# Local attention's scores from stacked high and low query parts, transposed two tiles ahead, and a weight's split and the conv's parts placed otherwise

## The chip, the cores and the metric

One Trainium2 chip, one of its cores. The metric is the device time of one execution in microseconds (us), given as a median over runs. Five engines work side by side in the core: TensorE (PE: matmuls and transposes; PEld is its weight load), VectorE (DVE), ScalarE (ACT), GpSimd (POOL) and SyncE (SP, which issues most DMAs). They meet at semaphores only.

## What is computed

Two transformer blocks, one behind the other, in float32. The change sits in the second block, between its input product and its output product:

```python
h = modulate(rmsnorm_2(x, g_mix[l]), sh1, sc1)
q, k, v, bg, cg, hv = jnp.split(h @ w_in[l], SPLIT_POINTS, axis=-1)
q = apply_rope(q.reshape(bsz, seq, N_HEADS, HEAD_DIM), cos, sin)      # 8 heads of 64
k = apply_rope(k.reshape(bsz, seq, N_KV_HEADS, HEAD_DIM), cos, sin)   # 2 heads of 64
att = windowed_attention(q, k, v, k_c, v_c, sink[l])  # 256 context keys, latent keys with |i-j| <= 128
conv = short_conv_mixer(bg, cg, hv, conv_w[l])        # bg * conv3(cg * hv)
x = x + gt1 * (jnp.concatenate([att, conv], axis=-1) @ w_out[l])
```

The 1024 tokens are 8 tiles of 128. A query tile sees 256 context keys, its own tile and the tile on each side: 640 keys for tiles 1 to 6, 512 for tiles 0 and 7. Four query heads share one key head.

## The kernel before

Every engine has its own instruction stream, written out by hand, so the order on an engine is the order of the code; waits are semaphores.

**Products in parts.** A float32 product is made of three passes in the type fp32r: each operand is split into a high part (ACT copies it to fp32r) and a low part (DVE subtracts the high part from the original), and `mm3` (L425 to L429) adds high*high, high*low and low*high. Weights come as blocks of 1024x512 into `raw`; `split_hi` (L402) makes `WH` in four pieces on ACT, `split_lo` (L417) makes `WL` in four pieces on DVE. There is one `WH` and one `WL`, so a piece is overwritten only when the last tile of the product before has used it (`w_used`). Activations lie as `AH` and `AL`.

**The input product of block two** runs as `gemm_tokens(B_I2, T_Q2)` for the queries (8 tiles), `gemm_tokens(B_I2 + 1, T_KV)` for keys and values (10 tiles, two of them context) and `gemm_pair` for the parts of the short convolution (T_CG, T_HV, T_BG). On DVE `rotate_tile` (L1656) rotates 8 query tiles (r 0 to 7) and 10 key tiles (r 8 to 17) into a two-deep buffer `QR`; beside the products `rot_transpose` (L2208) transposes them on TensorE and `rot_copy` (L1170) stores them on ACT: queries as `QT2` (two heads stacked per column block), keys as `KZ4`, each key head twice with zeros in the other 64 rows, so that one product over 128 rows gives one head. A tile of `QR` is free again when its transposes are done, and in `rotate_tile` DVE waits for that.

**The attention** (PE L2266 to L2322, ACT L1210 to L1234, DVE L1736 to L1769) is one loop over v, one head of one tile per turn. On TensorE turn v holds: the transposes of head v-2's probabilities (L2278, 5 of them, 4 in tiles 0 and 7); the scores of head v (L2287 over the context keys, L2288 over the own tile, L2292 over a side tile with L2293 for its mask) in plain float32; for v = 2 mod 8 the transposes of a tile's inverse sums (L2301); and a quarter of the product of probabilities and values (L2317). DVE takes the maximum (L1743, L1745), ACT the exponential (L1220). The transposed probabilities go through one pair of PSUM banks and are copied out by ACT for even v and by DVE for odd v (`probs_copy`, L570). At v = 6 mod 8 (from 14) DVE scales a finished tile's output out of PSUM (L1764).

**Between the two**, on DVE: `split_lo(B_W2)` for the output weight (L1727), the last of the products with bg (L1731), and `AL` of the convolution (L1734); on ACT `split_hi(B_W2)` (L1204) and `AH` of it (L1207), and a wait until DVE's part is done (L1209) before the first head.

Of the kernel before, what the change touches and what calls it, by code (L numbers as in the profile page):

```python
# [102 lines left out]
def build(nc, x, mem, positions, norm_mix_w, w_in, conv_w, conv_b, conv_ln_w, conv_ln_b, ret_gn_w, w_out,  # L103
# [123 lines left out]
    QT2 = at("w_q_T", [P, 4, S], F32, O_R + 32 * K + 512)  # L227
    KZ4 = at("w_k_T", [P, 4, CTX + S], F32, O_R + 48 * K + 512)
# [65 lines left out]
    with ExitStack() as stack:  # L294
# [107 lines left out]
        def split_hi(b, off=0, width=512):  # L402


            for j in range(4):
# [11 lines left out]
        def split_lo(b, off=0, width=512):  # L417

            for j in range(4):
# [124 lines left out]

        def key_slot(j):
            return 2 + j if j < NT else j - NT
# [64 lines left out]
        def residual_pe(b, n0, ni):  # L611
# [28 lines left out]
            sem("xa_" + s) for s in ("scores", "max", "exp", "probs", "probs_T", "copied", "out", "hi", "lo"))  # L640
# [5 lines left out]
        rt_tp, rt_cp, kz_zero = sem("rot_transposed"), sem("rot_copied"), sem("k_zeroed_then_slots")  # L646
# [113 lines left out]
        def _(pool):  # L760
# [114 lines left out]
            pool.wait_ge(x_saved, 16 * NT)  # L875
            pool.wait_ge(nm_xn, N_CTX)
            pool.memset(KZ4[64:128, 0:4:2, :], 0.0).then_inc(kz_zero, 1)
            pool.memset(KZ4[0:64, 1:4:2, :], 0.0).then_inc(kz_zero, 1)
# [6 lines left out]
            pool.memset(AFFALL[:, :, :], -1.0).then_inc(u2_pad, 1)  # L885
# [63 lines left out]
        def _(act):  # L949
# [220 lines left out]
            def rot_copy(r):  # L1170

                act.wait_ge(rt_tp, r + 1)
                ps = BK[4 + r % 4]
                if r < 8:
                    act.activation(QT2[:, :, tok(r)], ps.rearrange("p (c n) -> p c n", c=4), ACT.Copy).then_inc(rt_cp, 1)
                    return
                act.wait_ge(kz_zero, 2)
                i_ = tok(key_slot(r - 8))
                act.activation(KZ4[0:64, 0, i_], ps[0:64, 0:P], ACT.Copy)
                act.activation(KZ4[0:64, 2, i_], ps[0:64, P:2 * P], ACT.Copy)  # L1180
                act.activation(KZ4[64:128, 3, i_], ps[64:128, 0:P], ACT.Copy)
                act.activation(KZ4[64:128, 1, i_], ps[64:128, P:2 * P], ACT.Copy).then_inc(rt_cp, 1)

            for r in range(15):
                if r == 2:
                    norm_hi(N_CTX, CTH[:, :, tok(0)])
                if r == 3:
                    split_hi(B_I2 + 1)
                if r == 4:
                    norm_hi(N_CTX + 1, CTH[:, :, tok(1)])  # L1190
                rot_copy(r)
            for m in range(8):
# [7 lines left out]
                if m < 3:  # L1200
                    rot_copy(15 + m)
            split_hi(B_I2 + 3)
            split_hi(B_I2 + 4)
# [107 lines left out]
        def _(dve):  # L1311
# [344 lines left out]
            def rotate_tile(r):  # L1656
                n = (T_Q2 if r < 8 else T_KV - 8) + r
                dve.wait_ge(acc_ready, n + 1)
                if r >= 2:
                    dve.wait_ge(rt_tp, r - 1)  # L1660
                if r >= 1:
                    dve.wait_ge(acc_dve, freed(n)[1] - 1)
                q = QR[:, r % 2, :]
                if r < 8:
# [3 lines left out]
                if r == 8:  # L1668
                    dve.wait_ge(kz_zero, 2)
# [815 lines left out]
```

## Time and profile before

| | us |
|---|---|
| median of 3 runs | 2669.22 (2668.21 to 2670.24) |
| the profiled execution | 2671.51 |
| its span in the profile | 2669.9 |
| input product of block two, attention, up to the output product | some 1490 to 1874 of the span |
| attention alone, first transposes to the output product | 1703.6 to 1874.2 |

The profiled execution's own time is 1.6 us over its span and 2.3 us over the median. The profile says, for one execution, when every instruction ran and what released it. A row of its timeline has the start, the duration, the engine, the line of the kernel and the operation with the names of its tiles; behind "x" stands how many instructions are merged, and in brackets how long the engine had been idle and what ended that. A float32 matmul shows as two MATMULs, an fp32r one and a transpose as one. Matmuls are pipelined, so the distance between two starts, and not the duration, is what one costs.

### The profile page before, as it was taken

The page shows a single profiled execution, that of the slowest core. Times are in us where ns is not written, and L with a number is a line of the kernel's source. Part 1 is how long each engine was busy: PE and PEld are TensorE (multiplying, and loading weights), DVE is VectorE, ACT ScalarE, POOL GpSimd, SP SyncE. Part 2 cuts the span into 40 slices and gives each one's busy share as a digit, 9 for nine tenths or more (in the row PEclk, how much of TensorE's full clock was granted, in tenths as well). Part 3 has the DMA queues.
Part 4 walks back from the last instruction along what each step waited for, and adds up shares of the span by engine and source line. Part 5 has one row for each costly group of instructions (what it writes and reads, how often), then busy time and mean ns, then how long its engine had stood idle before and what let it go on. Part 6 is the DMA issues. An engine that isn't in the chain of part 4 may idle for free. (4 is left out here: it accounts for less than half of the span.)

```text
span 2669.9 us, 30052 instructions
## 1 busy us (share of the span) xinstructions
PE 2528.8 (95%) x11886; PEld 1989.0 (74%) x11886; DVE 1460.4 (55%) x1924; ACT 925.3 (35%) x1480; POOL 203.2 (8%) x224
## 2 busy tenths in 40 slices
PE   6999899999999999999999999899985999999996
PEld 5787578878888787878878888777774766677663
DVE  5999745224344564445446733566357656655562
ACT  4233534334231212112214321444152545544452
POOL 1000320000000000000000100000112011010100
PEclk9999889999999999999999999899986999999998
DMA  4111022220011232323230410200255999999996
GB/s 144 58 45 44 32 87 72 95 95 9 32 66 61 80 110 83 101 85 110 79 110 32 166 32 16 79 1 1 99 211 209 340 359 366 370 374 359 359 360 220
DMA packets 116260, 370.53 MB, mean 139 GB/s; under 512 B 6293, under 2 KB 15557, under 8 KB 116160
## 3 DMA queue, kind: packets, MB, share of 16 engines
q1 hardware_dynamic: 94688, 293.63, 29.6%
q0 software_dynamic: 21472, 75.51, 9.0%
q8 instruction: 70, 1.15, 0.2%
q14 instruction: 30, 0.25, 0.0%
HBM read 343.89 MB, written 25.26 MB: 138 GB/s over the span
## 5 line engine op out<-in xcount | busy, mean ns | idle before, releaser
L427 PE MATMUL banks<-act_hi,w_hi 128*128 128x512 f32 x960 | 376.6, 392 | 12.1 <-DVE act_lo L541 5.6
L1900 DVE TENSOR_TENSOR expert_w_lo<-expert_w,expert_w_hi 128x2048 fp32r<-128x2048 f32 x120 | 269.3, 2287 | 210.7 <-ACT expert_w_hi L1268 210.5
L429 PE MATMUL banks<-act_hi,w_lo 128*128 128x512 f32 x960 | 374.4, 390 | 0.0
L428 PE MATMUL banks<-act_lo,w_hi 128*128 128x512 f32 x960 | 374.4, 390 | 0.0
L1268 ACT ACTIVATE expert_w_hi<-expert_w 128x2048 fp32r<-128x2048 f32 x128 | 237.6, 1904 | 125.4 <-DMA expert_w<-in_w_gate 76.3
L414 ACT ACTIVATE w_hi<-w_raw 128x1024 fp32r<-128x1024 f32 x152 | 156.8, 1060 | 345.2 <-PE banks L429 345.1
L427 PE MATMUL banks<-w_hi,act_hi 128*128 128x512 f32 (+1 forms) x640 | 247.4, 387 | 10.0 <-DVE w_lo L421 6.3
L421 DVE TENSOR_TENSOR w_lo<-w_raw,w_hi 128x1024 fp32r<-128x1024 f32 x152 | 181.3, 1223 | 136.3 <-ACT w_hi L414 132.0
L429 PE MATMUL banks<-w_hi,act_lo 128*128 128x512 f32 (+1 forms) x640 | 244.7, 382 | 0.0
L428 PE MATMUL banks<-w_lo,act_hi 128*128 128x512 f32 (+1 forms) x640 | 244.2, 382 | 0.0
L427 PEld LDWEIGHTS banks<-act_hi,w_hi 128*128 128x128 f32 x960 | 180.8, 188 | 52.7 <-DVE act_lo L541 5.7
L429 PEld LDWEIGHTS banks<-act_hi,w_lo 128*128 128x128 f32 x960 | 180.7, 188 | 37.9
L2393 PE MATMUL banks<-expert_w,expert_hidden_T 128*128 128x512 f32 x480 | 208.5, 592 | 0.0
L428 PEld LDWEIGHTS banks<-act_lo,w_hi 128*128 128x128 f32 x960 | 180.9, 188 | 36.9
L427 PE MATMUL banks<-expert_w_hi,expert_rows_T_hi 128*128 128x512 f32 x512 | 203.6, 398 | 4.2 <-DVE expert_rows_T_lo L1904 4.2
L427 PE MATMUL banks<-w_hi,hidden_hi 128*128 128x512 f32 x512 | 201.3, 393 | 2.8 <-DVE w_lo L421 2.8
L429 PE MATMUL banks<-expert_w_hi,expert_rows_T_lo 128*128 128x512 f32 x512 | 201.6, 394 | 0.0
L428 PE MATMUL banks<-expert_w_lo,expert_rows_T_hi 128*128 128x512 f32 x512 | 201.2, 393 | 0.0
L428 PE MATMUL banks<-w_lo,hidden_hi 128*128 128x512 f32 x512 | 199.4, 390 | 0.0
L429 PE MATMUL banks<-w_hi,hidden_lo 128*128 128x512 f32 x512 | 199.3, 389 | 0.0
L1612 DVE TENSOR_TENSOR x_tokens<-x_tokens,banks 128x512 f32<-128x512 f32 x128 | 87.6, 686 | 166.8 <-PE banks L429 165.5
L2393 PEld LDWEIGHTS banks<-expert_w,expert_hidden_T 128*128 128x128 f32 x480 | 90.1, 190 | 107.7 <-issue 107.6
(382 smaller groups left out, 3892.0 us busy)
## 6 DMA issues: line engine op xcount, KB each, us to landing
expert_w<-in_w_gate SPq DMA_DIRECT2D x32, 2048.0 KB, 9.8
expert_w<-in_w_up SPq DMA_DIRECT2D x32, 2048.0 KB, 9.9
expert_w<-in_w_down SPq DMA_DIRECT2D x32, 2048.0 KB, 7.9
ada_w<-in_w_ada POOLq DMA_DIRECT2D x48, 512.0 KB, 4.2
w_raw<-in_mlp_up_w SPq DMA_DIRECT2D x16, 1024.0 KB, 5.4
w_raw<-in_mlp_down_w SPq DMA_DIRECT2D x16, 1024.0 KB, 5.1
w_raw<-in_w_in SPq DMA_DIRECT2D x10, 1024.0 KB, 5.3
w_raw<-in_w_in SPq DMA_DIRECT2D x18, 512.0 KB, 6.2
```

What stands on the lines that cost most here:

```text
L414: nc.scalar.activation(WH[:, 2 * j:2 * j + 2, 0:width], raw[:, half, 2 * (j % 2):2 * (j % 2) + 2, 0:width], ACT.Copy).then_inc(w_hi, 1)
L421: nc.vector.tensor_tensor(WL[:, 2 * j:2 * j + 2, 0:width], raw[:, j // 2, 2 * (j % 2):2 * (j % 2) + 2, 0:width], WH[:, 2 * j:2 * j + 2, 0: ...
L427: nc.tensor.matmul(o_, lh, rh, start=start, stop=False)
L428: nc.tensor.matmul(o_, lh, rl, start=False, stop=False)
L429: return nc.tensor.matmul(o_, ll, rh, start=False, stop=stop)
L1268: act.activation(EWH[slot][:, 2 * j:2 * j + 2, :], EW[slot][:, 2 * j:2 * j + 2, :], ACT.Copy).then_inc(w_hi, 1)
L1612: dve.tensor_tensor(xs, xs, acc(n), ALU.add).then_inc(acc_dve, 1)
L1900: dve.tensor_tensor(EWL[slot][:, c, :], EW[slot][:, c, :], EWH[slot][:, c, :], ALU.subtract).then_inc(w_ready, 1)
L2393: m = pe.matmul(PAIR[pair][:, 512 * half:512 * (half + 1)], lhs[:, k, :], EW[slot + k // 4][:, k % 4, 512 * half:512 * (half + 1)], start= ...
```

## The change

**Scores.** The rotated queries stay as rows (`QRT`). For each tile ACT copies them to fp32r (`query_hi`) and DVE subtracts (`query_lo`) into `QST`, in which each head's high and low parts stand side by side, 64 columns each. TensorE transposes that (`query_transpose`), so that a head's stationary operand has the high part in 64 rows and the low part in the other 64; ACT copies it into the free columns of `AH` and `AL` (`query_copy2`). Keys are split when they are rotated: `KHH` holds the high part twice, stacked, `KLO` the low part once. The scores are then two fp32r passes per stretch of keys: the stacked query against `KHH` (128 rows) and the query's high part against `KLO` (64 rows). The stretches are the 256 context keys, two neighbouring tiles (256 keys), and for tiles 1 to 6 a third tile (128 keys).

**Order.** Tiles 0 and 1 of the queries are prepared beside the last conv product, tile t + 2 within the attention of tile t. The context's transposes move into the query product, keys are transposed one tile sooner, zeroing of `KZ4` on POOL goes. The output weight's split is made in pieces at v = 4 to 11, the conv's parts in two halves, one before the first head and one at v = 2.

```diff
+        def query_parts(t, kv):
+            hi, lo = (slice(0, AD), slice(AD, P)) if kv == 0 else (slice(AD, P), slice(0, AD))
+            return QST[:, t % 2, 4 * kv:4 * kv + 4, hi], QST[:, t % 2, 4 * kv:4 * kv + 4, lo]
...
-            pool.wait_ge(c2_lo, 4)
+            pool.wait_ge(c2_lo, 2)
+            pool.memset(AFFALL[:, :, :], -1.0).then_inc(u2_pad, 1)
+            pool.wait_ge(qs_tp, QS0 + 2 * NT)
             row(GT1[:, :], mod_d[0, 2 * D:3 * D], mod_in)
...
+            def query_hi(t):
+                act.wait_ge(acc_dve, freed(T_Q2 + t)[1])
+                if t >= 2:
+                    act.wait_ge(qs_tp, QS0 + 2 * (t - 1))
+                for kv in range(2):
+                    i_ = act.activation(query_parts(t, kv)[0], query_rows(t)[:, 4 * kv:4 * kv + 4, :], ACT.Copy)
+                i_.then_inc(qs_hi, 1)
+            def query_copy2(t, kv, bank):
+                act.wait_ge(qs_tp, QS0 + 2 * t + kv + 1)
+                act.activation((AL if kv else AH)[:, 0:4, tok(t)], BK[bank].rearrange("p (c n) -> p c n", c=4),
+                               ACT.Copy).then_inc(qs_cp, 1)
...
-            split_hi(B_W2)
-            act.wait_ge(acc_dve, freed(T_BG + 7)[1])
-            for c in range(4):
-                act.activation(AH[:, 4 + c, :], C2[:, c, :], ACT.Copy).then_inc(c2_hi, 1)
-            act.wait_ge(c2_lo, 4)
+            act.wait_ge(acc_ready, T_BG + 6)
+            for t in range(2):
+                for kv in range(2):
+                    query_copy2(t, kv, 4 + 2 * t + kv)
+            conv_hi(0)
+            act.wait_ge(acc_ready, T_BG + 8)
+            conv_hi(1)
             for v in range(64 + 15):
+                if v == 2:
+                    act.wait_ge(c2_lo, 2)
+                if v in (4, 6, 8, 10):
+                    split_hi(B_W2, js=((v - 4) // 2,))
+                if v % 8 == 5 and v < 48:
+                    query_hi(v // 8 + 2)
+                if v % 8 in (0, 2) and 8 <= v < 56:
+                    t = v // 8 - 1
+                    query_copy2(t + 2, v % 8 // 2, 6 + (t + 1) % 2)
...
+            def query_lo(t):
+                dve.wait_ge(qs_hi, QS0 + t + 1)
+                for kv in range(2):
+                    hi, lo = query_parts(t, kv)
+                    i_ = dve.tensor_tensor(lo, query_rows(t)[:, 4 * kv:4 * kv + 4, :], hi, ALU.subtract)
+                i_.then_inc(qs_lo, 1)
...
             for v in range(64 + 16):
+                if v == 2:
+                    conv_lo(1)
+                if v in (5, 7, 9, 11):
+                    split_lo(B_W2, js=((v - 5) // 2,))
+                if v % 8 == 6 and v < 48:
+                    query_lo(v // 8 + 2)
...
             for v in range(64 + 11):
+                if v % 8 in (7, 1) and 7 <= v < 50:
+                    t, kv = (v - 7) // 8, (v - 7) % 8 // 2
+                    if t >= 1:
+                        pe.wait_ge(at_on, t)
+                    if kv == 1:
+                        pe.wait_ge(qs_cp, QS0 + 2 * (t + 2) + 1)
+                    query_transpose(t + 2, kv, 6 + (t + 1) % 2)
...
-                    pe.matmul(ps[:, 0:CTX], q, kz[:, 0:CTX], start=True, stop=True)
-                    m = pe.matmul(ps[:, CTX:CTX + P], q, kz[:, CTX + t * P:CTX + (t + 1) * P], start=True, stop=True)
-                    sides = ([(t - 1, 0)] if t > 0 else []) + ([(t + 1, 1)] if t < NT - 1 else [])
-                    for n, (kt, side) in enumerate(sides):
-                        dst = ps[:, CTX + P * (n + 1):CTX + P * (n + 2)]
-                        pe.matmul(dst, q, kz[:, CTX + kt * P:CTX + (kt + 1) * P], start=True, stop=False)
-                        m = pe.matmul(dst, IDB[:, :], MKB[:, side, :], start=False, stop=True)
+                    for dst, key, n in spans:
+                        beside = [i for i, kt in enumerate(near) if kt != t and dst <= CTX + P * i < dst + n]
+                        pe.matmul(ps[:, dst:dst + n], q, KHH[:, kv, key:key + n], start=True, stop=False, skip_group_check=True)
+                        m = pe.matmul(ps[:, dst:dst + n], q[part, :], KLO[part, key:key + n], start=False, stop=not beside,
+                                      skip_group_check=True)
+                        for i in beside:
+                            m = pe.matmul(ps[:, CTX + P * i:CTX + P * (i + 1)], IDB[:, :], MKB[:, int(near[i] > t), :], start=False,
+                                          stop=True, skip_group_check=True)
```

**How it moves instructions.** The lines of the changed kernel have their own numbers. First DVE, at the end of the query product, where it stands before the split of the key weight. Before:

```order
L1652 TENSOR_TENSOR rotated<-rotary_tmp 128x8x32 [waits dve_link]
L1653 TENSOR_TENSOR rotated<-rotary_tmp 128x8x32
L421 TENSOR_TENSOR w_lo<-w_raw,w_hi 128x1024 [waits w_hi_made] x4
L1648 TENSOR_TENSOR rotary_tmp<-banks,consts_sb 128x256 [waits acc_free_dve,rot_transposed,acc_ready]
L1649 TENSOR_TENSOR rotary_tmp<-banks,consts_sb 128x256
L1650 TENSOR_TENSOR rotary_tmp<-banks,consts_sb 128x256
L1651 TENSOR_TENSOR rotary_tmp<-banks,consts_sb 128x256
L1652 TENSOR_TENSOR rotated<-rotary_tmp 128x8x32 [waits dve_link]
L1653 TENSOR_TENSOR rotated<-rotary_tmp 128x8x32
L541 TENSOR_TENSOR ctx_lo<-banks,ctx_hi 128x4x128 [waits nm_hi] x2
```

and changed:

```order
L1693 TENSOR_TENSOR w_q_rows<-rotary_tmp 128x8x32 [waits dve_link]
L1694 TENSOR_TENSOR w_q_rows<-rotary_tmp 128x8x32
L545 TENSOR_TENSOR ctx_lo<-banks,ctx_hi 128x4x128 [waits nm_hi] x2
L425 TENSOR_TENSOR w_lo<-w_raw,w_hi 128x1024 [waits w_hi_made] x4
L1689 TENSOR_TENSOR rotary_tmp<-banks,consts_sb 128x256 [waits acc_free_dve,acc_ready]
L1690 TENSOR_TENSOR rotary_tmp<-banks,consts_sb 128x256
L1691 TENSOR_TENSOR rotary_tmp<-banks,consts_sb 128x256
L1692 TENSOR_TENSOR rotary_tmp<-banks,consts_sb 128x256
L1693 TENSOR_TENSOR w_q_rows<-rotary_tmp 128x8x32 [waits dve_link]
L1694 TENSOR_TENSOR w_q_rows<-rotary_tmp 128x8x32
```

The second context tile's low part has moved ahead of the split, and a query's rotation waits for no transposes any more.

Next DVE at the entry of the attention. Before:

```order
L1731 TENSOR_TENSOR short_conv_out<-short_conv_out,banks 128x512 [waits acc_ready] x4
L421 TENSOR_TENSOR w_lo<-w_raw,w_hi 128x1024 [waits w_hi_made] x4
L1731 TENSOR_TENSOR short_conv_out<-short_conv_out,banks 128x512 [waits acc_ready]
L1734 TENSOR_TENSOR act_lo<-short_conv_out,act_hi 128x1024 [waits short_conv_hi] x4
L1743 TENSOR_REDUCE w_max<-banks 128x1 [waits wa_scores]
L1745 TENSOR_SCALAR w_minus_max<-w_max,minus_sink 128x1 [waits dve_link]
```

and changed:

```order
L1791 TENSOR_TENSOR short_conv_out<-short_conv_out,banks 128x512 [waits acc_ready] x4
L1782 TENSOR_TENSOR act_lo<-short_conv_out,act_hi 128x4x512 [waits short_conv_hi]
L1791 TENSOR_TENSOR short_conv_out<-short_conv_out,banks 128x512 [waits acc_ready]
L1810 TENSOR_REDUCE w_max<-banks 128x1 [waits wa_scores]
L1812 TENSOR_SCALAR w_minus_max<-w_max,minus_sink 128x1 [waits dve_link]
L1810 TENSOR_REDUCE w_max<-banks 128x1 [waits wa_scores]
L1812 TENSOR_SCALAR w_minus_max<-w_max,minus_sink 128x1 [waits dve_link]
L1782 TENSOR_TENSOR act_lo<-short_conv_out,act_hi 128x4x512 [waits short_conv_hi]
```

The split of the output weight no longer stands ahead of the last product with bg, and of the conv's low part only half stands ahead of the first maximum.

Last TensorE in the loop, at a turn v = 7 mod 8. Before:

```order
L2278 MATMUL banks<-consts_sb,w_probs 128x128 [waits wa_copied_act,wa_exp]
L2278 MATMUL banks<-consts_sb,w_probs 128x128 x4
L2287 MATMUL banks<-w_k_T,w_q_T 128x256 [waits wa_exp]
L2288 MATMUL banks<-w_k_T,w_q_T 128x128
L2292 MATMUL banks<-w_k_T,w_q_T 128x128
L2293 MATMUL banks<-masks_bf_65,identity_bf_64 128x128
L2292 MATMUL banks<-w_k_T,w_q_T 128x128
L2293 MATMUL banks<-masks_bf_65,identity_bf_64 128x128
L2317 MATMUL banks<-w_probs_T,w_v 64x256 x2
```

and changed:

```order
L2315 MATMUL banks<-consts_sb,w_q_parts_f_135 128x128 [waits xa_max_then_query_lo,wa_normed]
L2315 MATMUL banks<-consts_sb,w_q_parts_f_135 128x128 x3
L2345 MATMUL banks<-consts_sb,w_probs 128x128 [waits wa_copied_act,wa_exp]
L2345 MATMUL banks<-consts_sb,w_probs 128x128 x4
L2363 MATMUL banks<-w_k_hi_T,act_lo 128x256 [waits wa_exp]
L2364 MATMUL banks<-w_k_lo_T,act_lo 128x256
L2363 MATMUL banks<-w_k_hi_T,act_lo 128x256
L2364 MATMUL banks<-w_k_lo_T,act_lo 128x256
L2367 MATMUL banks<-masks_bf_65,identity_bf_64 128x128
L2363 MATMUL banks<-w_k_hi_T,act_lo 128x128
L2364 MATMUL banks<-w_k_lo_T,act_lo 128x128
L2367 MATMUL banks<-masks_bf_65,identity_bf_64 128x128
```

Four float32 products became six fp32r passes, and ahead of them stand four transposes that wait for DVE's scaling of the finished tile (`wa_normed`).

## Rows read from the trace of the kernel before

**Rows 1.** The profile page's first line on engines: busy time, share, instructions.

```profile
PE 2528.8 (95%) x11886; PEld 1989.0 (74%) x11886; DVE 1460.4 (55%) x1924; ACT 925.3 (35%) x1480; POOL 203.2 (8%) x224
```

**Rows 2.** TensorE's waits from 1490 to 1930 us: total, times, longest.

```profile
PE banks L2278 <- ACT w_probs L1220: 5.8, 3, 4.6
PE banks L427 <- DVE w_lo L421: 3.6, 1, 3.6
```

**Rows 3.** Timeline at the start of the key product (start, us, engine, line).

```profile
1521.58 1.06 ACT L414 ACTIVATE w_hi<-w_raw 128x1024 fp32r<-128x1024 f32 x1 [0.24 <-PE banks L429]
...
1522.07 0.42 DVE L1648 TENSOR_TENSOR rotary_tmp<-banks,consts_sb 128x256 f32<-128x256 f32 x1 [2.82 <-PE banks L2218]
...
1524.20 4.62 DVE L421 TENSOR_TENSOR w_lo<-w_raw,w_hi 128x1024 fp32r<-128x1024 f32 x4
...
1526.61 0.57 PE L427 MATMUL banks<-w_hi,act_hi 128*128 128x256 f32 x1
...
1530.13 0.28 PE L428 MATMUL banks<-w_lo,act_hi 128*128 128x256 f32 x1
...
1530.25 0.28 PE L429 MATMUL banks<-w_hi,act_lo 128*128 128x256 f32 x1
```

**Rows 4.** Timeline at the entry of the attention, all engines.

```profile
1694.14 0.68 DVE L1731 TENSOR_TENSOR short_conv_out<-short_conv_out,banks 128x512 f32<-128x512 f32 x1
...
1694.97 1.19 PE L2287 MATMUL banks<-w_k_T,w_q_T 128*128 128x256 f32 x2 [3.10 <-DVE short_conv_out L1731]
...
1695.94 4.63 DVE L1734 TENSOR_TENSOR act_lo<-short_conv_out,act_hi 128x1024 fp32r<-128x1024 f32 x4 [1.12 <-ACT act_hi L1207]
...
1701.50 1.28 ACT L1220 ACT_TABLE_LOAD   x1 [2.75 <-DVE w_minus_max L1745]
...
1703.62 1.11 PE L2278 MATMUL banks<-consts_sb,w_probs 128*128 128x128 f32 x4 [4.59 <-ACT w_probs L1220]
```

**Rows 5.** Timeline of TensorE over one head in tile 2.

```profile
1750.00 0.22 PE L2293 MATMUL banks<-masks_bf,identity_bf 128*128 128x128 bf16 x1
...
1750.73 0.76 PE L2278 MATMUL banks<-consts_sb,w_probs 128*128 128x128 f32 x5
...
1751.34 0.60 PE L2287 MATMUL banks<-w_k_T,w_q_T 128*128 128x256 f32 x2
...
1752.69 0.65 PE L2317 MATMUL banks<-w_probs_T,w_v 128*64 128x256 f32 x4
...
1753.28 0.76 PE L2278 MATMUL banks<-consts_sb,w_probs 128*128 128x128 f32 x5
```

**Rows 6.** Timeline of DVE and ACT over the heads beside it.

```profile
1750.26 0.82 DVE L1743 TENSOR_REDUCE w_max<-banks 128x1 f32<-128x640 f32 x1 [1.47 <-PE banks L2293]
...
1751.12 0.21 DVE L1745 TENSOR_SCALAR w_minus_max<-w_max,minus_sink 128x1 f32<-128x1 f32 x1
...
1751.37 0.79 ACT L1220 ACTIVATE w_probs<-banks,w_minus_max 128x640 f32<-128x640 f32 x1 [0.90 <-DVE w_minus_max L1745]
...
1754.08 0.70 ACT L1212 ACTIVATE w_probs_T<-banks 128x640 f32<-128x640 f32 x1 [1.83 <-PE banks L2278]
...
1754.68 0.79 ACT L1220 ACTIVATE w_probs<-banks,w_minus_max 128x640 f32<-128x640 f32 x1
...
1756.34 0.68 DVE L1764 TENSOR_TENSOR w_out_T<-banks,w_inverse_sums_T 128x512 f32<-128x512 f32 x1
```

**Rows 7.** Timeline in tile 0, where TensorE waited for an exponential.

```profile
1709.58 0.68 ACT L1220 ACTIVATE w_probs<-banks,w_minus_max 128x512 f32<-128x512 f32 x1
...
1710.41 0.66 PE L2278 MATMUL banks<-consts_sb,w_probs 128*128 128x128 f32 x4 [0.42 <-ACT w_probs L1220]
```

**Rows 8.** Busy time by stretch there: PE, PEld, DVE, ACT, POOL, then granted clock.

```profile
1708.00:1710.00 2.00, 1.99 (x16) 1.56 (x15) 1.04 (x3) 1.25 (x4) 0.00 (x0) 1.00 0.00 0
```

**Rows 9.** Timeline of TensorE: the transposes of heads 8 and 56.

```profile
1720.99 0.77 PE L2278 MATMUL banks<-consts_sb,w_probs 128*128 128x128 f32 x5
...
1850.01 0.66 PE L2278 MATMUL banks<-consts_sb,w_probs 128*128 128x128 f32 x4
```

More of the change, by code:

```diff
@@ L400, in sp_load, with split_hi @@
             nc.sync.dma_start(raw[:, half, :, 0:width], src).then_inc(w_raw[half], 16)
-        def split_hi(b, off=0, width=512):
-            for j in range(4):
+        def split_hi(b, off=0, width=512, js=range(4)):
+            for j in js:
                 half = j // 2
@@ L415, in split_hi, with split_lo @@
                                      ACT.Copy).then_inc(w_hi, 1)
-        def split_lo(b, off=0, width=512):
-            for j in range(4):
+        def split_lo(b, off=0, width=512, js=range(4)):
+            for j in js:
                 nc.vector.wait_ge(w_hi, off * 4 + 4 * b + j + 1)
@@ L639, in build @@
         xa_s, xa_m, xa_e, xa_p, xa_t, xa_pt, xa_o, xa_hi, xa_lo = (
-            sem("xa_" + s) for s in ("scores", "max", "exp", "probs", "probs_T", "copied", "out", "hi", "lo"))
+            sem("xa_" + s) for s in ("scores", "max_then_query_lo", "exp_then_query_hi", "probs", "probs_T_then_query_T",
+                                     "copied_then_query_copied", "out", "hi", "lo"))
+        qs_lo, qs_hi, qs_tp, qs_cp, QS0 = xa_m, xa_e, xa_t, xa_pt, 16
         u_sq, u_hi, u_lo = sem("hidden_squared"), sem("hidden_hi_made"), sem("hidden_lo_made")
@@ L1168, in _, with key_copy @@
                     norm_hi(N_B2 + t - 2, a_hi(t - 2))
[L1170 to L1191, printed above, removed]
+            def key_copy(j):
+                act.wait_ge(rt_tp, j + 1)
+                if j == 0:
+                    act.wait_ge(x_saved, 16 * NT)
+                    act.wait_ge(nm_xn, N_CTX)
+                ps = BK[4 + j % 4]
+                i_ = tok(key_slot(j))
+                act.activation(KHH[:, :, i_], ps[:, 0:2 * P].rearrange("p (v n) -> p v n", v=2), ACT.Copy)
+                act.activation(KLO[:, i_], ps[:, 2 * P:3 * P], ACT.Copy).then_inc(rt_cp, 1)
+            norm_hi(N_CTX, CTH[:, :, tok(0)])
+            norm_hi(N_CTX + 1, CTH[:, :, tok(1)])
+            split_hi(B_I2 + 1)
+            for j in range(8):
+                key_copy(j)
             for m in range(8):
@@ L2264, in _, with query_transpose, first_queries2 @@
             gemm_pair(B_I2 + 3, T_BG, 256, False, True)
-            gemm_pair(B_I2 + 4, T_BG + 4, 0, True, True)
-            pe.wait_ge(rt_cp, 18)
+            def query_transpose(t, kv, bank):
+                pe.wait_ge(qs_lo, QS0 + t + 1)
+                for n in range(4):
+                    m = pe.transpose(BK[bank][:, n * P:(n + 1) * P], QSF[:, t % 2, 4 * kv + n, :], IDN)
+                m.then_inc(qs_tp, 1)
+            def first_queries2(m):
+                if m == 1:
+                    pe.wait_ge(rt_cp, 10)
+                    for t in range(2):
+                        for kv in range(2):
+                            query_transpose(t, kv, 4 + 2 * t + kv)
+            gemm_pair(B_I2 + 4, T_BG + 4, 0, True, True, after=first_queries2)
             pe.wait_ge(acc_dve, freed(T_BG + 7)[1])
+            pe.wait_ge(qs_cp, QS0 + 4)
             for v in range(64 + 11):
+                if v % 8 in (7, 1) and 7 <= v < 50:
+                    t, kv = (v - 7) // 8, (v - 7) % 8 // 2
+                    if t >= 1:
+                        pe.wait_ge(at_on, t)
+                    if kv == 1:
+                        pe.wait_ge(qs_cp, QS0 + 2 * (t + 2) + 1)
+                    query_transpose(t + 2, kv, 6 + (t + 1) % 2)
                 if 2 <= v <= 65:
@@ L2299, in _ @@
                         pe.wait_ge(at_on, t)
+                    if t + 2 < NT:
+                        pe.wait_ge(qs_cp, QS0 + 2 * t + 6)
                     for n in range(4):
@@ L2312, in _ @@
                             pe.wait_ge(at_on, t - 1)
-                    keys = [0, 1, 2 + t] + ([1 + t] if t > 0 else []) + ([3 + t] if t < NT - 1 else [])
+                    keys = [0, 1] + [2 + kt for kt in local_tiles(t)]
                     more = len(keys) - 4
```

164 lines of the change are left out of this document (85 added, 79 removed).

## The prediction

> **What bounds the kernel now.** The page's engine line [rows 1] has TensorE busy for 95% of the span, so time can come from its work or from its few stops. The table of waits for the part that the change touches [rows 2] shows the stops: 5.8 us for exponentials, nearly all of it once, at the entry of the attention, and 3.6 us for the low part of a weight. The timelines give the rest. At the key product [rows 3] ACT had the last high part done at 1522.64, but DVE began the low parts only at 1524.20: it had stood idle for 2.82 us until a transpose on TensorE freed the rotated buffer, and then rotated first. After the stop TensorE ran at half its clock: from 1526.61 to 1530.13 are 17 passes, 0.21 us each, where the next one costs 0.12. At the entry [rows 4] the last product with bg stood behind a weight's split, then the conv's low parts (4.63 us) stood ahead of the first maximum, and the first transposes came at 1703.62, though the product had ended at 1691.87.
>
> Within the attention one turn takes 2.55 us of TensorE's stream [rows 5]: transposes 0.61, scores 1.35 (with masks and the switch to the next line), values 0.59. It is unbroken there. The loop behind it [rows 6] has mask to maximum 0.26, maximum to the next step 0.86, that 0.21, and an ACT copy that starts 0.80 behind the transposes, with the next exponential 0.60 behind the copy. From an exponential's start to the transposes it releases [rows 7] are 0.83 for 512 keys, so 0.94 for 640 (the exponential takes 0.79 instead of 0.68) [rows 6, 7]. From head 8 to head 56 pass 129.0 us [rows 9], 21.5 for each of six full tiles.
>
> All sums are against the profiled execution, 2671.5; the median is 2.3 lower, and that I take off at the end.
>
> **1. Start of the key product: -4.1.** The rotation of a query no longer waits for transposes, and both context tiles' low parts stand ahead of the split. DVE then follows ACT piece by piece and is done one piece (4.62/4 = 1.2) after 1522.64, at 1523.9. TensorE finds the first piece ready: the 3.6 goes [rows 2], and with it the half clock, 17 x 0.21 - 17 x 0.12 = 1.5. New: 0.4 until the fourth piece, and 0.6 because keys are transposed one tile sooner, with two rotations (2.2 each, six steps of some 0.4 [rows 3]) and the key's own still queued on DVE.
>
> **2. Transposes beside the products: -0.7.** 32 of queries and 20 of keys go, 30 of keys and 16 of queries come, six fewer at 0.12 (0.61 for five) [rows 5]. Splitting keys on DVE replaces two small copies by two operations of similar size; each key tile has some 3 us of TensorE over it and DVE needs about 2.2, so this costs nothing; were that cover gone, 10 x 0.3. POOL's zeroing had ended long before; its two row loads now wait for the last query transposes, still 50 us ahead of their use. SP's load of the last weight half starts some 15 us later, 150 us ahead of its use: nothing.
>
> **3. Entry of the attention: -7.5.** The last product with bg starts when the matmul ends, 1691.9 instead of 1694.14, and TensorE 0.83 later [rows 4], 1692.7. The first maximum waits for no conv part: it and its successor are done at 1694.5. ACT does half of the conv's high part first (2048 elements, two of the 1.06 [rows 3], to 1694.6), then the 1.28 of table load and the 0.83 [rows 7]: transposes at 1696.7, 6.9 sooner. Behind it stand new pieces: 2.3 of conv on DVE before the third maximum (half of 4.63), and from v = 4 to 11 four splits of 1.06 on ACT and 1.2 on DVE, plus the first query tile's parts. Walked through turn by turn, they fill idle time of both engines for the most part and delay four turns by 0.3 to 0.7; shorter scores give back a little more. I take 7.5 at head 8; bounds 5.5 and 8.5.
>
> **4. Full tiles: -7.** A head's scores become four fp32r passes over 256 keys at 0.12 [rows 3], two over 128, one mask at some 0.06 and the last mask with the switch at 0.15 (1750.00 to 1750.15) [rows 5]. No row shows an fp32r pass over 128 columns. From below it is half of 0.12; from above it is the float32 rate, 1.35 - 0.21 over five blocks of 128 = 0.23. I take 0.11, the row it is nearest to: a transpose, also 128 columns behind a load of its own weights, at 0.12. Scores are then 0.48 + 0.22 + 0.06 + 0.15 = 0.91, and TensorE's turn 2.11 (bounds 2.01 and 2.35).
>
> TensorE does not get all of it. In even turns ACT copies, then takes the exponential that the next transposes need: 0.80 + 0.60 + 0.94 = 2.34. So four odd turns take 2.11, two even ones 2.34, and two are longer by a double share of values (some 0.42), one of them also by the transposes of the inverse sums (0.48) and a wait for them of 0.2: 8.44 + 4.68 + 2.53 + 3.21 = 18.9 a tile. To this come two groups of four query transposes, 0.48 each. That at v = 1 mod 8 lies partly in ACT's turn and costs 0.25. That at v = 7 mod 8 waits for DVE to scale the finished tile out of the same bank. From the start of the turn that is 0.61 + 0.76 + 0.26 + 0.86 + 0.21 + 0.04 + 0.68 = 3.42, with a hop 3.5, where TensorE arrives at 2.53: a new wait of 0.95, and 0.48 behind it. It falls in five tiles: 5 x (0.25 + 1.43) = 8.4. Six tiles: 113.4 + 8.4 = 121.8 against 129.0. The bounds of the 128-column pass make it 118 or 130.5. The parts of the queries on ACT and DVE (some 1.9 and 0.9 a tile) stand where either engine waits 0.7 and more for scores; uncovered they would cost 2.8 x 5 = 14.
>
> For the narrow pass there is also a rule in the Trainium skill, TensorE: Matmul & The Clock Gate, under Back-to-back issue gap: streams of load and matmul pairs sustain about 81 ns each at 128 columns. By it scores would be 0.06 shorter and the gain 2 us larger. The transposes here cost 120, so the sum stays with the row.
>
> **5. Last tile: -1.5.** Its heads have no third block; by the same rates scores shrink by some 0.37, and four of eight turns are TensorE's. The tail behind it is not touched.
>
> **Sum:** 4.1 + 0.7 + 7.5 + 7 + 1.5 = 20.8. 2671.5 - 20.8 = 2650.7, and 2.3 less on the median: **2648.5**.
>
> **Rivals.**
> *Narrow passes at the float32 rate* (0.23): the full tiles give nothing, rather -1.5 back. For it: no row at 128 columns. Against: the 256-column passes run at one column per cycle, and nothing [rows 3] hints at a change. Time 2648.5 + 8.5 = 2657.
>
> *ACT and DVE as the new bound.* Parts of queries, splits and the scaling meet in the same turns, transposes wait for both, and a full tile stays at about 21.5. For it: even turns are ACT's already in my sum. Against: DVE sits idle 1.47 and ACT 1.83 between operations [rows 6], more than is added to a turn. Time 2648.5 + 7 = 2655.5; if the entry's pieces don't hide either, 2659.
>
> *Waits overlap better:* the scaling is ready when TensorE arrives, narrow passes at 0.06: 4.8 + 3.6 more, 2640.
>
> *Slower: half clock in the attention.* TensorE's turn gets stops it does not have now, 0.23 in even turns and 0.95 once a tile. If the granted clock falls to 1.2 GHz there, a turn of 2.11 doubles to some 4, a full tile costs 34 instead of 20.3, and six of them 82 more: 2730. It decides from a quarter of the attention at half clock, since 20.8/82 is that. Against it: in tile 0, in the two microseconds before a stop of 0.42 [rows 7] and after others like it, the clock granted was 1.00 [rows 8]; for it: stops of 3.6 and 4.6 were followed by half clock [rows 3, 4]. The Trainium skill speaks against the change here: TensorE: Matmul & The Clock Gate, A second HAM failure mode, says that a TensorE which idles briefly between groups of matmuls, cycling through PSUM banks, swings between full and half clock. By that rule the time is this rival's; the trace of tile 0 does not agree with it.
>
> *The change does nothing:* what TensorE saves, another wait takes, 2669. It needs both the entry and the loop to fail, which share no cause.
>
> **How the numbers follow.** Chances: forecast 0.52, narrow passes 0.12, ACT and DVE 0.20, better overlap 0.08, half clock 0.04, nothing 0.04. The likeliest case's own range, from the entry's bounds and a 128-column pass of 0.06 to 0.13, is 2643 to 2654. The range for 8 in 10 takes in the two cases above it and most of the one below: 2640 to 2660. A measurement of this kernel tells about 0.2% (5.3 us) from no change. All cases but the last two lie below 2663.9: faster 0.92, same 0.04, slower 0.04.
>
> **What would show it.** Step 1: no wait for the low part at the key product, granted clock 1.00 through it, DVE's split ending some 1.3 behind ACT's. Step 3: the first transposes some 5 us behind the end of the last bg product, where it was 11.8. Step 4: narrow passes 0.11 apart, scores 0.91, odd turns near 2.1, even near 2.3, and once a tile TensorE idle some 0.95, released by the scaling on DVE. Wrong: scores over 1.1 (narrow passes), turns over 2.5 with TensorE waiting for exponentials or copies (ACT and DVE), a granted clock under 0.95 in full tiles (half clock), or a key product that still stops.

## The result and the profile after

The kernel became slower. Its median is 2715.07 us (2713.05 to 2717.88, 4 runs) against 2669.73 (2668.21 to 2671.43, 4 runs) of the kernel before on the same chip: ratio 1.0173, 95% interval 1.016 to 1.0186. Forecast were 2648.5 us, range 2640 to 2660, and 0.92 for faster. The profiled execution took 2717.88 us, its span is 2716.3, 46.4 more than the 2669.9 of before.

The page of the changed kernel, engine line and granted clock in 40 slices:

```profile
PE 2581.0 (95%) x11800; PEld 2002.4 (74%) x11800; DVE 1468.8 (54%) x1936; ACT 930.3 (34%) x1482; POOL 193.6 (7%) x222
...
PEclk9999889999999999999999999599996999999998
```

TensorE's share is still 95% [rows 1], with more busy time, and one slice of the clock stands at 5. The waits of TensorE for the same part as [rows 2]:

```profile
PE banks L2315 <- DVE w_out_T L1831: 3.0, 4, 0.8
PE banks L431 <- DVE act_lo L1835: 2.3, 1, 2.3
PE banks L2345 <- ACT w_probs L1261: 2.1, 2, 1.3
PE banks L2378 <- DVE w_inverse_sums L1825: 1.0, 1, 1.0
PE banks L2363 <- DVE short_conv_out L1791: 0.8, 1, 0.8
PE banks L431 <- DVE w_lo L425: 0.3, 1, 0.3
```

The two waits that the prediction wanted gone are gone: 3.6 for the low part became 0.3, 5.8 for exponentials became 2.1. TensorE waits less than before and yet needs longer, so the time is in what it executes. The timeline at the start of the key product, the place of [rows 3]:

```profile
1523.07 2.52 DVE L425 TENSOR_TENSOR w_lo<-w_raw,w_hi 128x1024 fp32r<-128x1024 f32 x2 [0.19 <-ACT w_hi L418]
1523.28 1.06 ACT L418 ACTIVATE w_hi<-w_raw 128x1024 fp32r<-128x1024 f32 x1 [0.24 <-PE banks L433]
1525.65 0.39 PE L431 MATMUL banks<-w_hi,act_hi 128*128 128x256 f32 x1 [0.26 <-DVE w_lo L425]
```

DVE follows ACT piece by piece, and the one stop left is 0.26. At the entry of the attention, the place of [rows 4]:

```profile
1688.28 0.69 DVE L1791 TENSOR_TENSOR short_conv_out<-short_conv_out,banks 128x512 f32<-128x512 f32 x1 [2.55 <-PE banks L433]
...
1689.02 0.38 PE L2363 MATMUL banks<-w_k_hi_T,act_hi 128*128 128x256 f32 x1 [0.78 <-DVE short_conv_out L1791]
...
1690.98 1.28 ACT L1261 ACT_TABLE_LOAD   x1
...
1693.11 0.69 PE L2345 MATMUL banks<-consts_sb,w_probs 128*128 128x128 f32 x2 [1.35 <-ACT w_probs L1261]
```

The last bg product starts when the matmul ends, the scores 0.74 behind it, and the first transposes come 4.8 behind the start of that product, at 1693.11 where it was 1703.62. Up to here the change is 10.5 us ahead, although its query product ended 1.7 later in this execution (1522.85 for 1521.15, last start); from there on it is 12.2. Now the scores of one head at full clock, with the weight loads (PEld):

```profile
1763.29 0.19 PEld L2363 LDWEIGHTS banks<-w_k_hi_T,act_hi 128*128 128x128 f32 x1
1763.32 0.36 PE L2363 MATMUL banks<-w_k_hi_T,act_hi 128*128 128x256 f32 x1
...
1763.61 0.18 PEld L2364 LDWEIGHTS banks<-w_k_lo_T,act_hi 64*128 64x128 f32 x1
1763.61 0.38 PE L2364 MATMUL banks<-w_k_lo_T,act_hi 64*128 64x256 f32 x1
1763.92 0.19 PEld L2363 LDWEIGHTS banks<-w_k_hi_T,act_hi 128*128 128x128 f32 x1
1763.92 0.38 PE L2363 MATMUL banks<-w_k_hi_T,act_hi 128*128 128x256 f32 x1
1764.23 0.18 PEld L2364 LDWEIGHTS banks<-w_k_lo_T,act_hi 64*128 64x128 f32 x1
1764.24 0.38 PE L2364 MATMUL banks<-w_k_lo_T,act_hi 64*128 64x256 f32 x1
```

The passes stand 0.29 to 0.32 apart, not 0.12. The load of each weight starts together with its own matmul, so none is hidden beside the pass before it, and each is 0.18 to 0.19 long: 0.12 + 0.19 = 0.31. The narrow passes (128 columns) stand 0.23 to 0.26 apart, with the same late loads. The next turn, whole, from its transposes to the values (1766.70 to 1769.73):

```profile
1767.22 0.36 PE L2363 MATMUL banks<-w_k_hi_T,act_hi 128*128 128x256 f32 x1
...
1769.15 0.65 PE L2394 MATMUL banks<-w_probs_T,w_v 128*64 128x256 f32 x4
1769.73 0.33 PE L2345 MATMUL banks<-consts_sb,w_probs 128*128 128x128 f32 x1
```

Its scores take 1.93, where 0.91 was forecast and 1.35 was the time before [rows 5]; the turn 3.03. A full tile at full clock takes 27.2 (head 16 starts at 1762.80, and the next four steps of eight heads are 27.2 each) where it took 21.5 [rows 9]; the first, mostly at half clock, takes 38.2 and the last, without query transposes, 24.5. Busy time by stretch, the last columns being granted clock, DMA share and GB/s:

```profile
1560.00:1680.00 120.00, 120.00 (x542) 99.57 (x541) 37.82 (x42) 23.52 (x33) 0.00 (x0) 1.00 0.14 44
1692.00:1720.00 28.00, 26.75 (x87) 17.29 (x88) 15.44 (x26) 13.42 (x31) 0.31 (x1) 0.51 0.12 38
1720.00:1752.00 32.00, 32.00 (x110) 19.39 (x110) 11.81 (x23) 9.44 (x20) 0.00 (x0) 0.50 0.10 33
1756.00:1870.00 114.00, 111.00 (x657) 72.06 (x653) 60.64 (x119) 51.44 (x115) 0.91 (x2) 1.00 0.00 1
```

From 1693 to 1753 the clock is at 1.2 GHz, behind the entry's stops, and it stays there although TensorE is without a stop in the last 32 of these microseconds. In the kernel before it fell at the same place and came back to full after some 14 us (1693.9 to 1707.6). The balance in the trace: up to the first transposes -10.5; head 0 to head 8 31.5 for 17.4, +14.2; head 8 to head 56 171.4 for 129.0, +42.4; the last tile +1.7; the rest -1.4. Together +46.4.

### The profile page after: what moved, and what is told of

The parts are those of the page before. It is cut to its first block, busy times and chain, and to the rows that moved or that the text cites. A ratio compares the mean times of both kernels' runs of the same rounds, so it can differ in the third digit from the quotient of the medians.

```text
span 2716.3 us, 29901 instructions
## 1 busy us (share of the span) xinstructions
PE 2581.0 (95%) x11800; PEld 2002.4 (74%) x11800; DVE 1468.8 (54%) x1936; ACT 930.3 (34%) x1482; POOL 193.6 (7%) x222
## 3 DMA queue, kind: packets, MB, share of 16 engines
q8 instruction: 70, 1.15, 0.2%
## 4 chain that ended last, share of the span: by engine, by line
PE 86%; DVE 9%; ACT 2%; DMA 1%; issue 1%; POOL 1%; SPq 0%; DVEq 0%; ACTq 0%; POOLq 0%
PE banks L431 21%; PE banks L433 21%; PE banks L432 21%; PE banks L2470 8%; DVE conv_out L1421 4%; PE banks L2364 2%; PE banks L2345 2%; DVE w_lo L425 2%; PE banks L2394 2%; PE banks L2363 1%; PE banks L531 1%; PE banks L2213 1%; PE banks L2192 1%; ACT w_hi L418 1%; PE banks L2367 1%
## 5 line engine op out<-in xcount | busy, mean ns | idle before, releaser
L433 PEld LDWEIGHTS banks<-act_hi,w_lo 128*128 128x128 f32 x960 | 181.2, 189 | 38.2
```

What stands on the lines that cost most here:

```text
L433: return nc.tensor.matmul(o_, ll, rh, start=False, stop=stop)
```

## The experiments

**Theory A:** passes on 128 rows and on 64 rows alternate, and each change of the row count exposes a weight load. **Rivals:** an fp32r pass with a stationary operand of a different tile is slow as such, or 64 rows are; or the whole loss is the clock. Ratios are to the kernel before in the same series (2669.29 to 2669.78 in all three).

**The low pass on 128 rows** (adds to each score the product of the query's low part with the other key head's low part):

```diff
-   pe.matmul(ps[:, dst:dst + n], q[part, :], KLO[part, key:key + n], start=False, ...)
+   pe.matmul(ps[:, dst:dst + n], q, KLO[:, key:key + n], start=False, ...)
```

> The changed kernel with one difference: the second pass of the scores uses the whole stacked query and all 128 rows of the low keys, instead of 64 rows (it adds the product of the query's low part with the other head's low keys, a term of the size that three-pass products drop anyway). Theory A: the change between 128-row and 64-row passes keeps a pass's weight load from running beside the pass before it, 0.19 us each time. Then passes stand 0.12 (256 columns) and 0.11 (128 columns) apart, a head's scores take 0.91 instead of 1.92, a full tile some 20.3 instead of 27.2, and the half clock after the entry is short as before the change: 2642 to 2656. Theory B: fp32r passes with these operands are slow for another reason (narrow columns, the doubled high keys): scores stay over 1.6, time over 2700. Theory C: the long stretch at half clock comes from the entry alone, and stays: scores 0.91, but 15 to 20 us more, 2660 to 2668.

Measured: 2646.58 us (2645.24 to 2647.68, 5 runs), ratio to before 0.9918 (0.9904 to 0.9931). One operand's rows are all that differs from the changed kernel, and 68.5 us go. The timeline of one head in this kernel:

```profile
1731.78 0.36 PE L2363 MATMUL banks<-w_k_hi_T,act_hi 128*128 128x256 f32 x1
1731.86 0.19 PEld L2364 LDWEIGHTS banks<-w_k_lo_T,act_hi 128*128 128x128 f32 x1
1731.98 0.28 PE L2364 MATMUL banks<-w_k_lo_T,act_hi 128*128 128x256 f32 x1
1731.98 0.19 PEld L2363 LDWEIGHTS banks<-w_k_hi_T,act_hi 128*128 128x128 f32 x1
...
1732.10 0.28 PE L2363 MATMUL banks<-w_k_hi_T,act_hi 128*128 128x256 f32 x1
1732.10 0.19 PEld L2364 LDWEIGHTS banks<-w_k_lo_T,act_hi 128*128 128x128 f32 x1
1732.22 0.28 PE L2364 MATMUL banks<-w_k_lo_T,act_hi 128*128 128x256 f32 x1
...
1732.52 0.27 PE L2364 MATMUL banks<-w_k_lo_T,act_hi 128*128 128x128 f32 x1
...
1732.80 0.65 PE L2394 MATMUL banks<-w_probs_T,w_v 128*64 128x256 f32 x4
1733.38 0.33 PE L2345 MATMUL banks<-consts_sb,w_probs 128*128 128x128 f32 x1
```

Each load now starts 0.12 ahead of its matmul, beside the pass in front, and passes are 0.12 apart. Scores take 1.02 (1731.78 to 1732.80), this odd turn 2.12 (1731.26 to 1733.38), a full tile 20.2 (1731.26 to 1751.47).

**All passes of 128 rows first, then those of 64, then the masks**, per head. Here the start of a bank's second stretch stands ahead of the additions to its first, so some sums of the first are most likely left out (this was not looked into); instructions and their number are the same, and only the time is read from it.

```diff
-   for dst, key, n in spans: hi pass; lo pass; masks
+   for dst, key, n in spans: hi pass
+   for dst, key, n in spans: lo pass
+   for dst, key, n in spans: masks
```

> The changed kernel with the 128-row passes of a head first, then its 64-row passes, then its masks: two changes of the row count a head instead of six. Theory A (each change exposes a weight load): scores 1.92 less four times some 0.19, so 1.1 to 1.3, and the time near 2660 to 2680. If 64-row passes are slow in themselves, whatever stands before them: scores stay near 1.9 and the time near 2715.

Measured: 2658.75 us (one run). The timeline merges the groups:

```profile
1763.50 0.54 PE L2362 MATMUL banks<-w_k_hi_T,act_lo 128*128 128x256 f32 x3
...
1763.97 0.41 PEld L2365 LDWEIGHTS banks<-w_k_lo_T,act_lo 64*128 64x128 f32 x3
1763.97 0.56 PE L2365 MATMUL banks<-w_k_lo_T,act_lo 64*128 64x256 f32 x3
...
1764.67 0.65 PE L2397 MATMUL banks<-w_probs_T,w_v 128*64 128x256 f32 x4
```

Scores 1.17, with the same passes on 64 rows: two changes of the row count instead of six. The time is just under the 2660 to 2680 expected. 64 rows are not slow as such.

**Every pass on 64 rows** (leaves out the product of the query's low part with the key's high part):

```diff
-   pe.matmul(ps[:, dst:dst + n], q, KHH[:, kv, key:key + n], start=True, ...)
+   pe.matmul(ps[:, dst:dst + n], q[part, :], KHH[part, kv, key:key + n], start=True, ...)
```

> Every pass of the scores on 64 rows of the same half: the first pass leaves out the product of a query's low part with a key's high part. Masks (128 rows) and transposes stay. Theory A (it is the change of the row count between neighbours that exposes a weight load, not 64 rows as such): two neighbouring 64-row passes stand about 0.12 apart at full clock, only the passes beside a mask or a transpose (five changes in a full head instead of seven) keep 0.24 to 0.31; scores between those of the full-row kernel (1.02) and of the changed one (1.92), about 1.5; 2670 to 2700 us. Theory B (a 64-row pass is slow as such): all six passes at 0.24 to 0.31, scores near 1.9 or above; 2715 us or more.

Measured: 2674.07 us (one run). Timeline:

```profile
1740.97 0.38 PE L2363 MATMUL banks<-w_k_hi_T,act_hi 64*128 64x256 f32 x1
...
1741.19 0.28 PE L2364 MATMUL banks<-w_k_lo_T,act_hi 64*128 64x256 f32 x1
1741.19 0.18 PEld L2363 LDWEIGHTS banks<-w_k_hi_T,act_hi 64*128 64x128 f32 x1
1741.31 0.28 PE L2363 MATMUL banks<-w_k_hi_T,act_hi 64*128 64x256 f32 x1
1741.31 0.19 PEld L2364 LDWEIGHTS banks<-w_k_lo_T,act_hi 64*128 64x128 f32 x1
1741.42 0.28 PE L2364 MATMUL banks<-w_k_lo_T,act_hi 64*128 64x256 f32 x1
1741.63 0.10 PEld L2367 LDWEIGHTS banks<-masks_bf,identity_bf 128*128 128x128 bf16 x1
```

Two 64-row passes stand 0.12 apart and their loads are hidden again; only the step to the mask (128 rows) takes 0.21. The head from its transposes on takes 2.05 up to the values (1740.27 to 1742.32), 0.51 more than with all 128 rows (1731.26 to 1732.80), for four more changes: 0.13 each. Theory A held in all three. My count of five changes against seven in the expectation was off by one, they are four and six.

**The clock.** First, dummy passes of 512 columns into a free bank on top of the changed kernel, where TensorE stood idle at the entry:

```diff
+   for _ in range(4): dummy pass                      # ahead of the first scores
+   if v in (1, 2, 3): (10, 6, 4)[v - 1] dummy passes  # behind the scores
```

> The changed kernel with fp32r passes of 512 columns into an unused bank where TensorE waits at the entry of the attention (4 before the first head, 10, 6 and 4 behind the scores of heads 1, 2 and 3), so that it has no stop there. If the stops at the entry bring the half clock (theory C), it stays at 1.00 from 1690 us on, and the time falls by about 20 us less the 3 of the added passes, to 2690 to 2700, with full tiles still at 27.2. If it is the loop with its exposed weight loads that pulls the clock down, it falls all the same, a few us later, and the time stays at 2710 to 2720.

Measured: 2697.74 us (one run). The clock stays at 1.00 to 1700, is 0.59 in 1700 to 1710 and 0.73 in 1710 to 1720, and 1.00 behind that: some 14 us at half clock for 61, and 17 us less. The time is in the range of the expectation's first branch, but the clock did not do what that branch says: it fell all the same at 1701.8, behind a stop of 0.84 at 1700.60, and with the same thin passes (the low passes on 64 rows) behind it it was back after 14 us.

Then the low pass on 64 rows in some tiles only, on 128 in the others:

```diff
+   q[part, :] if t >= 2 else q     # one kernel: thin passes late
+   q[part, :] if t < 2 else q      # the other: thin passes early
```

> The low pass on all 128 rows in token tiles 0 and 1, on 64 rows from tile 2 on. If the long half-clock stretch of the changed kernel needed its thin passes right behind the entry's stops, the clock is back at full by about 1710 as in the full-row kernel and stays there; tiles 2 to 6 take 27.2 us each instead of 20.2, the last some 3.5 more: 2646.6 + 38.5 = 2685 us. If the thin passes bring half clock by themselves, it shows again in tiles 2 to 7 and the time is 2700 or more.

> The other way round: 64 rows in tiles 0 and 1, 128 from tile 2 on. By the same account it carries the whole half-clock stretch (to about 1754) and 7 us for each of two tiles: 2715.1 - 38.5 = 2677 us, of which some 20 are the clock. If the clock has nothing to do with the thin passes: 2646.6 + 10 = 2657 us.

Measured: late 2683.50, early 2676.76 us (one run each). Busy time and clock of late (first row) and of early (the other two):

```profile
1710.00:1870.00 160.00, 156.10 (x944) 101.89 (x943) 87.48 (x171) 72.99 (x164) 1.06 (x2) 1.00 0.05 14
```

```profile
1700.00:1750.00 50.00, 49.97 (x170) 30.99 (x170) 20.88 (x38) 17.72 (x38) 0.00 (x0) 0.50 0.13 43
...
1754.00:1870.00 116.00, 111.10 (x890) 84.01 (x890) 82.72 (x165) 68.65 (x156) 1.06 (x2) 1.00 0.04 10
```

Against the full-row kernel (2646.6), thin passes in tiles 2 to 7 cost 36.9 and leave the clock at 1.00; in tiles 0 and 1 they cost 30.2 and carry the whole half-clock stretch (61 us in this kernel too). The two sum to 67.1, the changed kernel has 68.5. Of the 30.2, some 12 are the passes themselves (eight heads with six changes at 0.15, eight with four), and the other 18, by subtraction, the clock. So the clock falls at the stops of the entry in every version without dummy passes, and the long stretch at half clock comes only where thin passes stand right behind these stops. From tile 2 on thin passes do not bring it down. They are not the whole condition, since in the kernel with dummy passes the same thin passes let it back after 14 us; what ends the stretch stays open.

**Single terms of the sum, on the full-row kernel.** The next weight's split and the second conv part ahead of the attention again:

```diff
-   in the loop: split_hi / split_lo(B_W2) one piece at v = 4 to 11, conv_lo(1) at v = 2
+   ahead of the loop: split_hi(B_W2), split_lo(B_W2), conv_lo(1)
```

> The full-row kernel with one part of the change undone: the next weight's split stands ahead of the attention on ACT and DVE again, and so does the second half of the conv's low part. The forecast gave the entry 7.5 us: of it 5 to 7.5 should come back, the first transposes 5 us or more later: 2652 to 2654 us. If these pieces cost the same inside the attention as ahead of it, the time stays at 2646.6.

Measured: 2648.15 us (2646.36 to 2650.69, 5 runs), ratio 0.9923 (0.991 to 0.9937), not to be told from the full-row kernel, and less than the 2652 to 2654 expected. In the trace, from the last pass of the bg product to head 0 it is 9.4 instead of 5.3 (4.1 lost, where 5 or more were expected), but to head 8 26.6 instead of 24.3.

The low parts for the key product behind the last two rotations again:

```diff
-   split_lo(B_I2 + 1); rotate_query(6); rotate_query(7)
+   rotate_query(6); rotate_query(7); split_lo(B_I2 + 1)
```

> The full-row kernel with the low parts for the key product made behind the last two rotations again, not ahead of them. The forecast put 4.1 us on this start (3.6 of waiting, 1.5 of half clock, less 1.0 of new waits). The stop for the low part should be back with 3 to 4 us and some half clock behind it: 2646.6 + 4 to 5.5 = 2651 us. If the key product's start was not on the path, the time stays.

Measured: 2648.15 us (2647.19 to 2650.57, 5 runs), ratio 0.9919 (0.9905 to 0.9933), where 2651 was expected. The stop is back:

```profile
1522.42 0.35 PE L431 MATMUL banks<-w_hi,act_hi 128*128 128x256 f32 x1 [3.53 <-DVE w_lo L425]
```

From the last pass of the query product to the last of the bg product are 170.2 instead of 165.0, 5.2 more. But from there to head 8 this execution needs 21.9 instead of 24.3, with a higher clock behind the entry (0.81, 0.76 and 1.00 in the three stretches of 4 us from 1692 on; the full-row kernel has 0.62, 0.80 and 0.77). Both undone terms are thus visible in their own place, and each is given back about half by head 8. Here it is the clock, at half for 3.4 us instead of 10.2. With the splits ahead it is not: behind head 0 the clock is at half for 8.3 us against 9.2 in the full-row kernel, about as long, so there the pieces that no longer stand in the turns are the likelier reason, which no run separates.

**Two tries for a better version.** The query transposes that waited for DVE's scaling behind that turn's scores:

```diff
-   if v % 8 in (7, 1): query transposes ahead of the turn's transposes
+   v % 8 == 1: as before; v % 8 == 7 (from 15): behind the turn's scores
```

> The full-row kernel, with the query transposes of v = 7 mod 8 issued behind that turn's scores instead of ahead of its transposes, from tile 1 on, so that the scaling on DVE is done when TensorE comes to them. The wait of 0.75 that stands five times in the trace should go: 3.7 us less, 2643 us, and a full tile at 19.5 instead of 20.2. If ACT or DVE are the bound of these turns, the wait only turns into one for exponentials or copies and the time stays at 2646.6.

Measured: 2644.84 us (2643.44 to 2646.21, 4 runs), ratio 0.9905 (0.989 to 0.9921). The wait is gone, head 8 to head 56 takes 115.2 for 119.3, 4.1 less where 3.7 was expected; the intervals of the two ratios overlap, so the times alone don't show it.

And with dummy passes over the entry's stops:

```diff
+   4 dummy passes ahead of the first scores
+   (0, 11, 2, 1, 3, 4)[v] dummy passes behind the scores of heads 0 to 5
```

> The kernel of the later query transposes with dummy passes of 512 columns into a free bank, 4 ahead of the first scores and 11, 2, 1, 3, 4 behind the scores of heads 1 to 5, where TensorE stood idle. The full-row kernel was granted 0.67 and 0.91 in 1690 to 1710, some 4 us of lost work. With the clock kept at 1.00: 2 to 4 us less than without dummy passes, 2640 us. If the passes come out longer than the stops that they fill, the gain is eaten up: 2643 us or more.

Measured: 2639.14 us (2638.44 to 2639.73, 4 runs), ratio 0.9885 (0.987 to 0.99). Clock by stretch:

```profile
1690.00:1700.00 10.00, 9.53 (x67) 7.06 (x65) 8.72 (x17) 8.62 (x20) 0.00 (x0) 1.00 0.01 2
```

It does not fall at the entry, and from the bg product to head 8 are 21.5 instead of 24.4, 3.0 less, as expected (2 to 4). The medians differ by 5.7, but the two profiled executions are already 3.9 apart at the end of the bg product, before the first dummy pass, so 3.0 is what the passes are seen to give. This version beats both kernels: 1.15% below before, 2.8% below the changed one.

## Why the prediction was wrong

**The step that failed** is in part 4: "four fp32r passes over 256 keys at 0.12 [rows 3], two over 128". The 0.12 came from passes that all use 128 rows. The low pass of this change uses 64, and no row of the kernel before has such a pass between passes of 128. The sum carried 0.12 and 0.11 over without a bound for that. Measured are 0.31 and 0.24, scores of 1.92 instead of 0.91: 1.0 a head, 7 us a full tile, 42 for six. The bounds I gave (0.06 to 0.23) were drawn for the column count, the wrong unknown; the row count had none.

A hint of the price stood in the rows. In [rows 5] the mask at 1750.00 is followed by the values at 1750.15, while a mask followed by scores took 0.06 (1749.67 to 1749.72):

```profile
1749.72 0.44 PE L2292 MATMUL banks<-w_k_T,w_q_T 128*128 128x128 f32 x2
1750.15 0.20 PEld L2317 LDWEIGHTS banks<-w_probs_T,w_v 128*64 128x64 f32 x4 [0.16 <-issue]
1750.15 0.65 PE L2317 MATMUL banks<-w_probs_T,w_v 128*64 128x256 f32 x4
```

Between mask and values the tile changes from 128*128 to 128*64, and the first load starts with its own matmul. I read this 0.15 as "the last mask with the switch" and took it into the scores once, and did not ask how many such switches the change adds. They are six a head. At 0.15 - 0.06 = 0.09 each (an estimate, since this is a change of columns and not of rows) they give 0.54, scores of 1.45 instead of 1.35 before, and the forecast's sign for the full tiles turns; at the 0.15 that is measured here ((1.92 - 1.02) / 6) they give the result. The Trainium skill states the rule, TensorEngine Tiling (Array Packing), Tiling Modes, Key Properties: changing the tiling mode, and not just the tile, drains TensorE. The traces agree as far as they go: at every change of the row count a load starts late, at 0.13 to 0.15 a change. This was the rule that spoke against the change, and the prediction did not draw on it.

**Part 1, right.** No stop but 0.26, clock 1.00 through the key product, DVE 1.3 behind ACT. With part 2 the forecast was 4.8; from the end of the query product to that of the bg product are 165.0 in the full-row kernel for 170.3 before, 5.3.

**Part 3, right up to head 0, then too large.** The first transposes came 4.8 behind the last bg product's start, as forecast. From the bg product's end to head 8 the full-row kernel needs 24.3 for 29.5, 5.2 instead of 7.5. The missing 2.3 are the clock: 0.67 in 1690 to 1700 and 0.91 behind it, which I had not priced. Three kernels have the same instructions in this stretch, with 10.2 us at half clock (full rows), 6.8 (thin passes late) and 3.4 (low parts behind), and need 24.3, 22.9 and 21.9; the last is 7.6 less than before. With dummy passes it is 21.5, a gain of 8.

**Part 4, without its failed step, right.** In the full-row kernel scores are 1.02 (forecast 0.91; the first pass behind a transpose costs 0.20 and the narrow one 0.14), the odd turn 2.12 (2.11), the even one bound by ACT 2.34 (2.34), and the new wait once a tile is there:

```profile
1741.20 0.66 PE L2315 MATMUL banks<-consts_sb,w_q_parts_f 128*128 128x128 f32 x4 [0.75 <-DVE w_out_T L1831]
```

0.75 instead of 0.95, in five tiles. Six tiles take 119.3, forecast 121.8. **Part 5:** head 56 to the last head 14.3 for 15.5, 1.3 (1.5). The whole comes to 2646.6 where 2648.5 was forecast (2648.4 by its own terms), from one row count. That the forecast is so near is in part luck: part 3 gave 2.3 too little and part 4, with 9.7 for 7, 2.7 more. The parts together give 21.5 in the trace (forecast 20.8), and another 3.7 lie outside them: the query product ended 2.2 sooner than in the kernel before, and behind the last head it is 1.5.

**The rivals.** That a narrow pass costs 0.23 came true in its number (0.24) and not in its cause, which also hit the wide passes. Half clock in the attention came true in part: its mechanism, stops that end in 1.2 GHz, was already at work at the entry, and with thin passes behind it it lasted 61 us, for a cost of some 18. I had put 82 us and a chance of 0.04 on it, and my evidence against it [rows 8] was two microseconds in tile 0. The rule of the Trainium skill quoted there (TensorE: Matmul & The Clock Gate, A second HAM failure mode), of a TensorE that idles briefly between groups and swings between both clocks, does not describe the stretch: in 1720 to 1752 TensorE was busy throughout and the clock did not swing. Nearer to it is the entry of the full-row kernel, with stops of 0.4 to 1.0 between its heads: half clock, then full from 1695.0 to 1698.4, half again to 1701.8, and full.

## What to carry to other kernels

Before a duration is carried from a row to a new operation, compare all of its shape: rows, columns of the stationary operand, and moving columns, and also what stands ahead of it. Count the changes of the stationary operand's shape in the new order; each costs a weight load that is otherwise hidden, some 0.15 us here, more than a 256-column pass (0.12). A product that is short of rows was cheaper here with harmless rows added (1.02 a head) than cut down to its own rows (1.92); grouped with its like it came close (1.17).

## What was unexpected of the hardware

- A change between stationary operands of 128 and 64 rows, either way, lets the weight load (0.18 to 0.19) start only with its own matmul: 0.31 for 0.12 at 256 columns, 0.24 for 0.12 to 0.14 at 128. Passes on 64 rows among themselves are as fast as on 128.
- After the stops at the entry the clock stayed at 1.2 GHz for 61 us with thin passes behind them (six changes of the row count a head), for 3 to 14 us in all with full ones. What in the thin passes keeps it down (the gaps for the loads, or the empty rows) was not separated. With 64 rows in all passes (four changes) it was at half for 17 us, and with grouped passes (two) for 20 us in two pieces, up to 1713.8; both have empty rows and fewer gaps, which speaks for the gaps. But with dummy passes ahead of them six changes a head had it down for only 14 us.
- Work without any use, 25 passes in the entry's stops, gained 3.0 us there (24.4 to 21.5 from the bg product to head 8), since the clock then did not fall at the entry.
